# A two-block transformer kernel on one core: some weight chunks are placed 64 bytes further into their slots

## What is computed

```
def swiglu(h, w_gu, w_down):
    g, u = jnp.split(h @ w_gu, 2, axis=-1)
    return (jax.nn.silu(g) * u) @ w_down
...
        x = x + 0.5 * mx[2][:, None] * swiglu(modulate(rms_norm(x), mx[0], mx[1]), ffn1_w_gu[layer], ffn1_w_down[layer])
        ctx = ctx + 0.5 * mc[2][:, None] * swiglu(modulate(rms_norm(ctx), mc[0], mc[1]), ffn1_w_gu[layer], ffn1_w_down[layer])
```

## Time and profile before

| | |
|---|---|
| Time, median of 3 runs | 2135.13 us (2134.06 to 2137.99) |
| The profiled execution's own time | 2135.54 us |
| Its span, first to last instruction | 2133.8 us |
| TensorE matmuls (PE) busy | 2047.1 us, 96% |
| TensorE weight loads (PEld) busy | 1707.6 us, 80% |
| VectorE (DVE) busy | 1424.0 us, 67% |
| ScalarE (ACT) busy | 694.3 us, 33% |
| Mean granted TensorE clock | 0.988 of full speed |

### The profile page before, as it was taken

One profiled execution on the slowest core, in us unless ns is written; L12 is line 12 of the kernel. 1 busy time (PEld: TensorE's weight loads), 2 busy tenths in 40 slices (PEclk: granted clock), 3 DMA queues, 4 the chain that ended last, 5 costly groups with the idle time before them and its releaser, 6 DMA issues.

```text
span 2133.8 us, 31334 instructions
## 1 busy us (share of the span) xinstructions
PE 2047.1 (96%) x13199; PEld 1707.6 (80%) x13199; DVE 1424.0 (67%) x1890; ACT 694.3 (33%) x962; POOL 245.0 (11%) x286
## 2 busy tenths in 40 slices
PE   8999988888999999999999999999999999999998
PEld 7989985554788888896798888889888888877887
DVE  6887553333788599356579668737866863767675
ACT  6554322112422122245532212123221222465453
POOL 1000003231100000400121000030000004010000
PEclk9999999899999999999999999999999999999999
DMA  9646769999665565332136456444645643415664
GB/s 279 207 171 205 240 238 375 411 412 404 205 194 173 158 199 161 111 99 65 40 99 197 138 168 178 126 121 145 197 136 166 185 124 116 138 46 158 175 179 120
DMA packets 384121, 387.14 MB, mean 181 GB/s; under 512 B 18041, under 2 KB 351342, under 8 KB 371566
## 3 DMA queue, kind: packets, MB, share of 16 engines
q1 hardware_dynamic: 355438, 304.31, 44.2%
q0 software_dynamic: 27952, 79.77, 12.1%
q10 hardware_dynamic: 592, 1.05, 0.1%
HBM read 430.68 MB, written 1.05 MB: 202 GB/s over the span
## 4 chain that ended last, share of the span: by engine, by line
PE 83%; DVE 8%; DMA 6%; ACT 2%; issue 1%; SPq 0%; POOL 0%; DVEq 0%; POOLq 0%; ACTq 0%
PE B L2020 22%; PE B L2022 21%; PE B L2021 21%; PE B L2525 6%; DMA WB<-in_w 5%; PE B L2526 3%; PE B L2473 2%; DVE LO L816 2%; PE B L2862 1%; DVE HF L1195 1%; PE B L2507 1%; PE B L2836 1%; PE B L2847 1%; DMA W<-in_w 1%; DVE hL L1183 1%
## 5 line engine op out<-in xcount | busy, mean ns | idle before, releaser
L2020 PE MATMUL B<-hH,HI 128*128 128x512 f32 (+1 forms) x1600 | 565.7, 354 | 4.1 <-DVE hL L1183 2.1
L2022 PE MATMUL B<-hH,LO 128*128 128x512 f32 (+1 forms) x1600 | 558.1, 349 | 0.0
L2021 PE MATMUL B<-hL,HI 128*128 128x512 f32 (+1 forms) x1600 | 557.9, 349 | 0.0
L816 DVE TENSOR_TENSOR LO<-RAW,HI 128x2048 fp32r<-128x2048 f32 (+3 forms) x218 | 443.2, 2036 | 93.7 <-ACT HI L1571 89.3
L1571 ACT ACTIVATE HI<-RAW 128x2048 fp32r<-128x2048 f32 (+3 forms) x218 | 368.8, 1694 | 335.9 <-PE B L2022 276.9
L2020 PEld LDWEIGHTS B<-hH,HI 128*128 128x128 f32 x1600 | 302.5, 189 | 47.9 <-DVE LO L816 4.7
L2021 PEld LDWEIGHTS B<-hL,HI 128*128 128x128 f32 x1600 | 302.6, 189 | 39.4 <-issue 1.2
L2022 PEld LDWEIGHTS B<-hH,LO 128*128 128x128 f32 x1600 | 302.5, 189 | 39.1
L904 DVE SCALAR_TENSOR_TENSOR MACC<-MADW,CS,MACC 128x1024 f32<-128x1024 f32 x224 | 277.5, 1281 | 9.4 <-DMA MADW<-in_ada_w 3.7
L2020 PE MATMUL B<-aH,HI 128*128 128x512 f32 (+1 forms) x605 | 221.0, 365 | 0.0
L2022 PE MATMUL B<-aH,LO 128*128 128x512 f32 (+1 forms) x605 | 220.2, 364 | 0.0
(11 more groups left out here) (425 smaller groups left out, 3174.2 us busy)
## 6 DMA issues: line engine op xcount, KB each, us to landing
RAW<-in_ffn_w_gu SPq DMA_DIRECT2D x176, 512.0 KB, 5.2
MADW<-in_ada_w POOLq DMA_DIRECT2D x128, 512.0 KB, 4.0
W<-in_w SPq DMA_DIRECT2D x31, 1024.0 KB
RAW<-in_w_in SPq DMA_DIRECT2D x60, 512.0 KB, 4.8
WB<-in_w SPq DMA_DIRECT2D x28, 1024.0 KB
RAW<-in_ffn_w_down SPq DMA_DIRECT2D x56, 384.0 KB, 3.7
RAW<-in_ffn_w_down SPq DMA_DIRECT2D x56, 320.0 KB, 4.2
WA<-in_w SPq DMA_DIRECT2D x17, 1024.0 KB
```

What stands on the lines that cost most here:

```text
L816: V.tensor_tensor(LO[s][:, :words], RAW[s][:, :words], HI[t.hi[s]][:, :words].bitcast(F32), ALU.subtract).then_inc(lo_done[s], 1)
L2020: mm(o, wh, xh, start=first, stop=False, **more)
L2021: mm(o, wh, xl, start=False, stop=False, **more)
L2022: return mm(o, wl, xh, start=False, stop=last, **more)
```

## The change

A table `PLACES` gives every chunk a pair of byte offsets, 0 or 64: where its high part lies in the HI slot, and where the raw data and the low part lie in the RAW slot. Chunks whose products have 256 columns get 64 for both (`BY_HALVES`), chunks whose products have 512 get 0 for both (`WHOLE`), and the chunks of the last FFN get 64 for the high part and 0 for the low (`ABREAST`). The slots grow by 256 bytes each, so their distances become 8448 bytes. The shared region begins at offset 142464, still a multiple of 256 from the start of the activations. The DMAs, the copies, the subtractions and the products use the views at the chunk's place. No instruction is added or taken away.

```
+LINE = 64
+SLOT = 4 * CHUNK + 4 * LINE
+BY_HALVES, WHOLE, ABREAST = (LINE, LINE), (0, 0), (LINE, 0)
+def chunk_places():
+    places = [BY_HALVES] * FIRST_CHUNKS
+    staggered = [BY_HALVES] * 2 + [WHOLE] * (2 * FT_HALF + 2 * len(DOWN_CHUNKS) - 2 - (KT - EVEN)) + [BY_HALVES] * (KT - EVEN)
+    places += staggered
+    places += [BY_HALVES] * 2 + [WHOLE] + [BY_HALVES] * 2
+    places += [WHOLE] * 2 + [BY_HALVES] * 2
+    places += staggered + staggered
+    places += [BY_HALVES] * 4 + [WHOLE]
+    places += [BY_HALVES] * 4
+    places += [ABREAST] * (2 * FT_HALF + 2 * len(DOWN_CHUNKS) - 1) + [BY_HALVES]
+    return places
...
         self.hi[s] = copy_slot(self.pos)
+        self.hi_at[s], self.lo_at[s] = PLACES[self.pos]
...
-        RAW = [sb(f"RAW{i}", [P, CHUNK]) for i in range(RAW_SLOTS)]
-        HI = [sb(f"HI{i}", [P, CHUNK], F32R) for i in range(FIRST_HI)]
+        cursor[0] += SLOT * (RAW_SLOTS + FIRST_HI)
+        def placed(name, dt, at0, i):
+            return {place: nc.alloc_sbuf_tensor_at(f"{name}{i}" if place == 0 else f"{name}{i}S", [P, CHUNK], dt,
+                                                   offset=at0 + place) for place in (0, LINE)}
+        RAW = [placed("RAW", F32, raw_at + SLOT * i, i) for i in range(RAW_SLOTS)]
+        LO = [placed("LO", F32R, raw_at + SLOT * i, i) for i in range(RAW_SLOTS)]
+        HI = [placed("HI", F32R, raw_at + SLOT * (RAW_SLOTS + i), i) for i in range(FIRST_HI)]
...
-        union = cursor[0] = (cursor[0] + P - 1) // P * P
+        union = cursor[0] = cursor[0] + (base - cursor[0]) % (4 * LINE)
...
-                V.tensor_tensor(LO[s][:, :words], RAW[s][:, :words], HI[t.hi[s]][:, :words].bitcast(F32),
+                at = t.lo_at[s]
+                V.tensor_tensor(LO[s][at][:, :words], RAW[s][at][:, :words], HI[t.hi[s]][t.hi_at[s]][:, :words].bitcast(F32),
                                 ALU.subtract).then_inc(lo_done[s], 1)
...
             def slot(s, **dims):
                 v = "p (k n) -> p k n"
-                return HI[t.hi[s]][:].rearrange(v, **dims), LO[s][:].rearrange(v, **dims)
+                return (HI[t.hi[s]][t.hi_at[s]][:].rearrange(v, **dims), LO[s][t.lo_at[s]][:].rearrange(v, **dims))
```

More of the change, by code:

```diff
@@ L117 @@
 EVEN = 6
+LINE = 64
[12 more added lines that the diff above has]
+    return places
+PLACES = chunk_places()
 START = {"gated": 1, "silu_ready": 1}
@@ L129, in __init__ @@
         self.pos = self.used = 0
-        self.hi = {}
+        self.hi, self.hi_at, self.lo_at = {}, {}, {}
     def at(self, key, back=0):
@@ L184, in build @@
         raw_at = cursor[0]
-        RAW = [sb(f"RAW{i}", [P, CHUNK]) for i in range(RAW_SLOTS)]
-        LO = [nc.alloc_sbuf_tensor_at(f"LO{i}", [P, CHUNK], F32R, offset=raw_at + 4 * CHUNK * i)
-              for i in range(RAW_SLOTS)]
-        HI = [sb(f"HI{i}", [P, CHUNK], F32R) for i in range(FIRST_HI)]
+        cursor[0] += SLOT * (RAW_SLOTS + FIRST_HI)
[5 more added lines that the diff above has]
+        HI = [placed("HI", F32R, raw_at + SLOT * (RAW_SLOTS + i), i) for i in range(FIRST_HI)]
         T = [sb(f"T{i}", [P, 512]) for i in range(6)]
@@ L239, in in_raw @@
             assert offset + n <= 4 * CHUNK
-            return nc.alloc_sbuf_tensor_at(name, shape, dt, offset=raw_at + 4 * CHUNK * slot + offset)
+            return nc.alloc_sbuf_tensor_at(name, shape, dt, offset=raw_at + SLOT * slot + offset)
         WA = [None, in_raw("WA1", 1, 0, [P, KT, S]), at(16, "WA2", [P, KT, S])]
-        WAHEAD = [nc.alloc_sbuf_tensor_at("WAHEAD0", [P, KT, S], F32, offset=raw_at + 4 * CHUNK * RAW_SLOTS),
+        WAHEAD = [nc.alloc_sbuf_tensor_at("WAHEAD0", [P, KT, S], F32, offset=raw_at + SLOT * RAW_SLOTS),
                   in_raw("WAHEAD1", 0, 0, [P, KT, S])]
         WB = [at(24 + 8 * c, f"WB{c}", [P, KT, S]) for c in range(3)]
-        FIRST_WA = nc.alloc_sbuf_tensor_at("FIRST_WA", [P, KT, S], F32, offset=raw_at + 4 * CHUNK * (RAW_SLOTS + 1))
+        FIRST_WA = nc.alloc_sbuf_tensor_at("FIRST_WA", [P, KT, S], F32, offset=raw_at + SLOT * (RAW_SLOTS + 1))
         FIRST_WB = XC[:, :, S:]
@@ L268, in build @@
         JUNK = R[1][:, 0:S]
-        YH, YL = HI[1][:, 0:D], HI[1][:, D:2 * D]
+        YH, YL = HI[1][0][:, 0:D], HI[1][0][:, D:2 * D]
         SIL, HID = T[0][:, 0:S], T[0][:, S:2 * S]
@@ L282, in build @@
         HF = at(45, "HF", [P, KT, S])
-        HI.append(at(75, "HI2", [P, CHUNK], F32R))
+        HI.append(placed("HI", F32R, union + 1024 * 75, 2))
         OUTB = at(0, "OUTB", [P, TB, D])
@@ L299, in build @@
         FW = at(69, "FW", [P, LAYERS, 2, S])
-        assert union + 1024 * 83 <= nc.sbuf_usable_end, (union + 1024 * 83 - nc.sbuf_usable_end)
+        assert union + 1024 * 83 + LINE <= nc.sbuf_usable_end, (union + 1024 * 83 + LINE - nc.sbuf_usable_end)
         h_at = [base + 4 * KT * 2 * S * i for i in (1, 2)]
@@ L460, in chunk @@
                 h0 = words[0]
-                sp.dma_start(RAW[s][:, 0:h0].rearrange("p (k n) -> p k n", n=first.shape[-1]), first)\
+                raw = RAW[s][t.lo_at[s]]
+                sp.dma_start(raw[:, 0:h0].rearrange("p (k n) -> p k n", n=first.shape[-1]), first)\
                     .then_inc(raw_loaded[s], 16)
-                sp.dma_start(RAW[s][:, h0:h0 + words[1]].rearrange("p (k n) -> p k n", n=second.shape[-1]), second)\
+                sp.dma_start(raw[:, h0:h0 + words[1]].rearrange("p (k n) -> p k n", n=second.shape[-1]), second)\
                     .then_inc(raw_loaded[s], 16)
@@ L1570, in prep @@
                 s = take()
-                A.activation(HI[t.hi[s]][:, :words], RAW[s][:, :words], ACT.Copy).then_inc(hi_done[s], 1)
+                A.activation(HI[t.hi[s]][t.hi_at[s]][:, :words], RAW[s][t.lo_at[s]][:, :words], ACT.Copy)\
+                    .then_inc(hi_done[s], 1)
             def root(mean, r):
@@ L2589, in ffn @@
                         b = 4 + m % (4 if n > S else 3)
-                        wh = HI[t.hi[s]][:, :ks * P].rearrange("p (k n) -> p k n", n=P)
-                        wl = LO[s][:, :ks * P].rearrange("p (k n) -> p k n", n=P)
+                        wh = HI[t.hi[s]][t.hi_at[s]][:, :ks * P].rearrange("p (k n) -> p k n", n=P)
+                        wl = LO[s][t.lo_at[s]][:, :ks * P].rearrange("p (k n) -> p k n", n=P)
                         if k0 == 0:
```

## The result

The change makes the kernel 0.55% faster. The median goes from 2134.99 us (6 runs, 2133.05 to 2137.99) to 2123.24 us (6 runs, 2122.41 to 2125.88), a ratio of 0.9945 with a 95% interval from 0.9935 to 0.9955. That is 11.75 us less. The direction was forecast, but the forecast was 2109, a gain of 25.9, and less than half of that came. The time fits the rival "half of it" (2122). The lines of the code have moved by some 33: `exact` is now lines 2053 to 2055, `abreast` 2558 and 2559, the subtraction 848 and the copy 1603. An S at the end of a tile's name is the view at 64 bytes.

The account below looks back on a forecast made before the run. It took the rate at which dense TensorE products start as the bound, with DMA in the expert stage. First block 10.2, second block 12.3 and last FFN 3.4 us gave 25.9 us, hence 2109 us, range 2099 to 2137.

Parts of the forecast that it names:

- half of it: Rival: moving-operand shift goes the other way, or only some loads gain; half the products gain, 13 us, to 2122; chance 0.15.
- TensorE's wait for experts' weights: Sign in the expert stage: TensorE's waits for experts' weights should grow by 1 to 2 us.
- the first block's last 192 products: First block's last four chunks: their lead only becomes a longer wait for experts' weights, so nothing was counted.
- one step of 6.67 ns down: Price of the 64 bytes: each counted 256-column product starts every 113.2 ns instead of 119.9.
- the second block: Products behind the first block: 1845 of 1965 count, those of five first tiles left out; 12.3 us gained.
- slower: Rival: products enter the state of the last FFN's second half, 3885 x 3.33 ns = 13 us, to 2148; chance 0.14.
- the load's pace: Rival: 256-column products fall to 112.4 ns, the upper bound; 31.4 us gained, to about 2104; chance 0.10.
- The last FFN's term: 517 pairs with the high part moved by 64 gain one step each, 3.4 us; pairs at 0.340 us at first.
- The conversion: From product gains to end time: 120 first-tile products left out, VectorE-busy attention from 98 to 170 us gives back 1.3 us.
- Nothing: Rival: the 13.3 ns are a fixed cost of changing weights, so the change does nothing, 2135; chance 0.16.

Follow-up runs that it names:

- slots alone: Changed kernel with its new slot spacing and shared region, but every chunk at offset 0: 2136.05 us, 1.0003 of before.
- the second trace of the same kernel: The changed kernel run once more, unaltered, beside the run with 64 bytes only in the first block: 2122.16 us, 0.9944 of before.
- the run with these alone: Changed kernel with the twelve moving-operand chunks at 192 instead of 64: 2120.15 us, 0.9934 of before.
- the combination: Changed kernel with moving-operand chunks and four chunks behind transitions at 192, chunk 180 and the last FFN's second half at (192, 0): 2116.97 us, 0.9915 of before.
- the last FFN at 0: Changed kernel with the last FFN's 39 chunks at 0 for both parts: 2122.46 us, 0.9948 of before.

## Why the prediction was right in direction and wrong in size

**The sign and the step's size were right.** The excess over the columns is 6.67 or 13.3 ns in the windows of 256-column products, and 64 bytes take one step away: 113.2 was forecast and 113.2 is measured in the window answering to the earlier trace rows. The "slots alone" run excludes the other parts of the change. The cost of the edit itself is nothing, as counted. The loads beside 256-column products went from 192 to 188 ns, as forecast, at 200 to 262 us:
```profile
L2053 PEld LDWEIGHTS B<-YAH,HI0S 128*128 128x128 f32 x48 | 9.0, 188 | 0.0
```
The subtraction kept its 2290 ns, also where its inputs stand at unequal offsets (1928 to 1985 us), answering to the earlier trace rows:
```profile
L848 DVE TENSOR_TENSOR LO<-RAW,HI1S 128x2048 fp32r<-128x2048 f32 x4 | 9.2, 2293 | 1.4 <-ACT HI1S L1603 1.2
```
TensorE's wait for experts' weights (WB) was to grow by 1 to 2 us, and it fell from 28.6 to 26.7 (27.3 in the second trace of the same kernel). That the experts would swallow what the first block's last 192 products gain is not borne out: the lead was 6.3 at 261 us, 7.3 at the end of the first block and 6.7 behind the experts, and in the second trace it grew in the experts, from 7.2 to 8.3.

**The step that failed is the price "one step of 6.67 ns down" for all 3573 counted products.** It holds for 2365 of the 3784 steps that could be read (of 3885 products), and the others go at 117.8, a third of a step below 120. On the traced products this is 18.6 us where one full step each would be 3784 x 6.67 = 25.2. The term that was most mis-sized by it is the second block, 12.3 forecast. I had seen two paces in the last FFN, and used them for the rival "slower" and for the load's pace, but not for the forecast: with two paces at one address before, I should have expected that a shifted address can have two as well.

**The last FFN's term, 3.4 us, was 0.5.** Its pairs left 346.7 and 353.3 for 350 throughout. The forecast 340 exists (the second run of the same kernel has it), but it was not reached in this execution.

**The conversion was mis-sized.** The sum left out 120 products and took 1.3 us off for the attention, some 2 us in all, besides the first block's last 192. Measured, 19.1 us on products become 11.5. In the first block 9.8 become 7.3 at its end (10.2 forecast). Most of the loss lies between 98 and 198 us, where the lead grows by 0.9 us while the products save 2.4 (1.3 was to be given back, and 1.5 was). VectorE is the busiest engine but TensorE there, and TensorE's waits for it grew. Run by itself, the first block brought 7.1 us. In the second part 9.3 become 4.7 (5.7 against the runs beside it), where 12.3 + 3.4 was forecast. Of the loss, 1.9 go in the second mixer, between 1833.7 and 1847.7 us (0.8 in the wait and 1.5 at half clock, less what is won back there). The rest goes a few tenths at a time, 1.5 in all, at first tiles, where activations set the start; that is read from the two traces, and no run isolates it. The half clock is in no term of the sum.

**The rivals.** "Nothing" fell with the step of 113.2. The Trainium skill's rule in "SBUF — State Buffer", section "Who interferes with whom", that TensorE's two read ports are independent and it never waits for anyone, does not agree with these runs in the way the prediction drew on it, that no shift of addresses changes anything. Moving the same bytes by 64 changes 256-column products from 120.0 to 113.3 ns and 512-column products from 226.7 to 233. Whether the ports themselves are the reason no run shows. "Slower" fell for 256 columns, but it is what happens to 512 columns, by one step for each product. "The load's pace" was not seen: no stretch is below 113.3, in any of the runs. The spacing that the Trainium skill gives in "TensorE: Matmul & The Clock Gate", section "Back-to-back issue gap", 109.2 ns for 256 columns by its formula, was not reached either. The page gives that formula for an isolated matmul and says that in a stream of loads and matmuls both set the spacing, so that the prediction asked more of it than it says. "Half of it" had the time. Its mechanism, that some products gain and others don't and that the direction of the shift counts, has part of the truth: in the first block and the first mixer moving-operand chunks are mostly at 117.8 at 64, and mostly at 113.3 at 192 in the run with these alone. But in the combination they are mostly slow at 192 too (132 of 374 steps in the first block at 113.3), and more than half of the changed kernel's slow products are weight chunks at the same 64 bytes as the fast ones, which is the pace and not the direction. That the time came out at 2122 as this rival had it is in part luck: its 13 us are half of the products at a full step and nothing lost, and measured are 2365 of 3784 at a full step, the others at a third of one, and some 7 us lost again.

**What stays open.** Why 64 bytes help 256 columns and hurt 512. Whether the distance of the two operands counts or each one's own address: all runs move the chunk and leave the activations where they are, and none moves both by the same bytes. What picks the pace when a stretch is entered: it repeats from execution to execution in the first block and not in the last FFN, and a turn falls on a chunk at another place only sometimes. Whether 192 is better for moving operands as such, since with it the weight chunks behind them got slower, and in the combination it helped fewer of them.

## What to carry to other kernels

Hold the time from one matmul's start to the next against columns over clock. If an excess stays, sweep the place of one operand in steps of 32 or 64 bytes for each width by itself: here the best place for 256 columns was the wrong one for 512. Read the pace stretch by stretch and in two executions, not from one window, because one address had two paces that each lasted for many chunks. And count what arrives: of 19 us saved on products on the engine that bounds the kernel, 11.5 reached the end in one execution, and of 20 us 14.9 in another.

## What was unexpected of the hardware

- At full clock (granted 1.00, 2.4 GHz) back-to-back 128x128 products of 256 columns start every 113.3, 117.8 or 120.0 ns, which is 6.7, 11.1 or 13.3 over their columns, those of 512 columns every 226.7 or, at 64 bytes, 233 (13.3 and 20 over), and the pairs every 340, 346.7, 350 or 353.3. No stretch lies closer to its columns than 6.7 ns a product.
- At 1.2 GHz the same products, at the same places, start every 213 ns, which is 256 columns at that clock with no excess at all.
- A pace once taken lasted over buffers and tens of microseconds (113.3 from 200 to 262 us, pairs at 350 from 1928 to 1985), until a wait, another kind of product or a chunk at another place. In the changed kernel's first block it repeated chunk by chunk in two executions.
- The half clock of 3.4 us in the second mixer came behind a wait of 2.08 us in the changed kernel. With the last FFN at 0, the same wait of 2.08 us had no half clock behind it. Before, the wait was 1.32 us and the clock stayed full. Of the eight traces with a wait of 2.1 us there, six have the half clock, and none of the five with 1.3 or 1.9 us.
